# Rebuilt attention with masks, column halves and scaled probabilities in a three-layer block

## The chip, the cores and the metric

The kernel runs on one core of a Trainium2 chip, in fp32 throughout (weights are split into a high and a low part, so that three products in the engine's faster fp32 form give one of full precision). The metric is the device time of the launch in microseconds, the median of the runs shown.

## The reference

256 tokens of width 1024 pass through a first block (recurrent branch and a gated attention of 16 heads, merged, then a feed-forward) and two more layers (a block attention and a latent attention, each with a feed-forward). At 256 tokens all three attentions come down to causal softmax; the gated one has a selected and a window branch over the same 256 tokens, and a compressed branch with 15 keys:

```python
out = gb[..., 0:1] * o_cmp + gb[..., 1:2] * o_slc + gb[..., 2:3] * o_win       # gated
s = jnp.einsum("bhqd,bhkd->bhqk", qi, k) * scale                               # latent, block
s = jnp.where(key_pos[None, :] <= qpos[:, None], s, NEG_INF)
p = jax.nn.softmax(s, axis=-1)
o = jnp.einsum("bhqk,bkhd->bqhd", p, v)        # then o.reshape(B, S, H * dh) @ w_o
```

## The kernel before

Five engine programs are written out by hand, one `@block` function each, and meet only by semaphores. Each engine works in order. The weights come as 356 chunks of 128 x 1024 (`weight_stream`), through a ring of three raw buffers and one of six split ones: ScalarE writes the high part (`split_high`, L1264), VectorE the low part (`split_low`, L1720), TensorE multiplies (`split_product`, L607 to L609). The chunk's split is thus a duty of both engines everywhere, also inside the attentions.

An attention (`attention` in each of the engine programs) runs over heads. For a head, TensorE forms scores of two query tiles (128 x 128 and 128 x 256) in one bank, adds the mask as a bf16 product of identity and mask (L744), VectorE takes the negative row maxima (L1788, L1789), ScalarE the exponents with their sums (L1331, L1333), TensorE turns the three tiles of probabilities (L753), VectorE copies them out (L1795), and TensorE multiplies them, as the stationary operand, with the values of 64 columns (L765 to L767). Four heads share a bank of outputs, which VectorE multiplies by the inverse sums (`output`, L1802 to L1814; in the gated attention also by the gate, and adds the branches up). At the end TensorE turns the outputs, 16 tiles for each attention (`turn_output`, L802), ScalarE and VectorE write their high and low parts, and the output projection follows. The scores of two heads are formed side by side in row halves of the engine in the gated and the block attention (L737, L739), not in the latent one (L726, L727).

Between the heads stands other work. In the gated attention (32 items: 16 heads, two branches) halves of the merge-gate chunks (`merge_gates`, `mg`), with VectorE's `merge_scaled`; ahead of it the compressed branch, whose sums start at L2112. In the block attention the query and key tiles (`query_or_key`, 12 of 16 inside), which ScalarE copies out (`rope_operand`, L1589), TensorE rotates (`turn_rope`, L1108) and VectorE combines (`rope`, L2177 to L2185, one behind each head). In the latent attention the products of queries and keys (`query_product`, `key_product`), read by ScalarE (L1653, L1648) and VectorE (`query_rope`, L2256).

## Time and profile before

| | us |
|---|---|
| runs | 1176.53, 1176.68, 1176.81 (median 1176.68) |
| span of the profiled execution | 1173.1 |
| TensorE busy | 1141.7 (97%) |
| VectorE busy | 899.5 (77%) |
| ScalarE busy | 686.4 (59%) |
| DMA, mean | 162 GB/s read from HBM |

Busy times are unions of instruction spans; a matmul's span runs on while the next has started, so what one costs is the distance from its start to the next one's. In a timeline, columns are start, duration, engine, line, operation, result and operands with shapes, count, and in brackets idle time before and who ended it. A window's row gives its length and for each engine busy time and count, then the granted clock, the share of the DMA engines and GB/s.

### The profile page before, as it was taken

How to read it: one execution, taken by the hardware profiler on the slowest of the kernel's cores; microseconds unless marked ns; L12 is line 12 of the kernel's file. 1: busy time of each engine (PE TensorE's matmuls, PEld its weight loads, DVE VectorE, ACT ScalarE, POOL GpSimd, SP SyncE). 2: the span in 40 equal slices, each digit the busy share in tenths (PEclk: the TensorE clock that was granted, in tenths of full speed). 3: DMA queues.
4: the chain of work that ended last, by engine and by line, in shares of the span. 5: the costliest groups of instructions: out<-in, count | busy, mean ns of one | idle time of the engine just before them, and what ended most of it. 6: DMA issues, size and time to landing. Idle time of an engine off the chain costs nothing.

```text
span 1173.1 us, 25426 instructions
## 1 busy us (share of the span) xinstructions
PE 1141.7 (97%) x9673; PEld 1108.9 (95%) x9673; DVE 899.5 (77%) x1550; ACT 686.4 (59%) x1210; POOL 10.2 (1%) x13
## 2 busy tenths in 40 slices
PE   6999999999999999999999999999999999999997
PEld 6999999989999999999899899999998899999997
DVE  5788778678787998888777768776787777877774
ACT  6768764544556676556654456555565846655554
POOL 1000000000001000000000000000000000000000
PEclk9998999999999999999999999999999999999999
DMA  6675644521164676666453246766644423776661
GB/s 237 199 210 165 189 131 152 174 89 55 55 181 128 218 224 204 194 196 192 159 158 111 72 139 213 217 195 189 193 144 141 127 73 127 223 215 195 191 197 37
DMA packets 52923, 190.82 MB, mean 163 GB/s; under 512 B 6000, under 2 KB 6256, under 8 KB 52848
## 3 DMA queue, kind: packets, MB, share of 16 engines
q1 hardware_dynamic: 52416, 188.64, 52.5%
q8 instruction: 54, 0.88, 0.3%
q10 hardware_dynamic: 432, 1.12, 0.2%
q14 instruction: 21, 0.17, 0.0%
HBM read 188.69 MB, written 1.05 MB: 162 GB/s over the span
## 4 chain that ended last, share of the span: by engine, by line
PE 80%; DVE 8%; ACT 5%; DMA 4%; issue 2%; SPq 0%; DVEq 0%; ACTq 0%
PE bank L607 23%; PE bank L608 22%; PE bank L609 22%; DMA w_raw<-weight_stream 4%; DVE w_low L1720 3%; ACT w_high L1264 2%; PE bank L753 1%; DVE arena L1968 1%; PE bank L766 1%; PE bank L767 1%; PE bank L615 1%; PE bank L617 1%; PE bank L616 1%; PE bank L765 1%; PE bank L739 1%
## 5 line engine op out<-in xcount | busy, mean ns | idle before, releaser
L1720 DVE TENSOR_TENSOR w_low<-w_raw,w_high 128x1024 fp32r<-128x1024 f32 x356 | 434.6, 1224 | 148.0 <-ACT w_high L1264 144.2
L1264 ACT ACTIVATE w_high<-w_raw 128x1024 fp32r<-128x1024 f32 x356 | 375.1, 1058 | 265.3 <-PE bank L609 178.1
L607 PE MATMUL bank<-h_high,w_high 128*128 128x256 f32 x1760 | 495.1, 281 | 11.8 <-DVE h_low L1758 10.5
L608 PE MATMUL bank<-h_low,w_high 128*128 128x256 f32 x1760 | 488.5, 278 | 0.0
L609 PE MATMUL bank<-h_high,w_low 128*128 128x256 f32 x1760 | 488.5, 278 | 0.0
L607 PEld LDWEIGHTS bank<-h_high,w_high 128*128 128x128 f32 x1760 | 331.7, 188 | 13.7 <-issue 10.5
L608 PEld LDWEIGHTS bank<-h_low,w_high 128*128 128x128 f32 x1760 | 331.9, 189 | 0.4
L609 PEld LDWEIGHTS bank<-h_high,w_low 128*128 128x128 f32 x1760 | 331.7, 188 | 0.0
L607 PE MATMUL bank<-r_high,w_high 128*128 128x256 f32 x942 | 265.5, 282 | 3.8 <-ACT arena L1653 2.1
L608 PE MATMUL bank<-r_low,w_high 128*128 128x256 f32 x942 | 261.5, 278 | 0.0
L609 PE MATMUL bank<-r_high,w_low 128*128 128x256 f32 x942 | 261.5, 278 | 0.0
L607 PEld LDWEIGHTS bank<-r_high,w_high 128*128 128x128 f32 x942 | 177.9, 189 | 9.8 <-ACT arena L1653 3.6
L608 PEld LDWEIGHTS bank<-r_low,w_high 128*128 128x128 f32 x942 | 177.8, 189 | 0.2
L609 PEld LDWEIGHTS bank<-r_high,w_low 128*128 128x128 f32 x942 | 177.7, 189 | 0.0
L1846 DVE SCALAR_TENSOR_TENSOR arena<-arena,small 128x255 f32<-128x255 f32 (+1 forms) x184 | 87.9, 478 | 5.7 <-ACT arena L1359 2.4
L1331 ACT ACTIVATE arena<-bank,stats 128x128 f32<-128x128 f32 x64 | 23.4, 365 | 54.1 <-DVE stats L1789 53.9
L1359 ACT ACTIVATE arena<-arena,small 128x256 f32<-128x256 f32 x68 | 40.0, 589 | 13.7 <-DVE arena L1860 13.6
L1744 DVE TENSOR_TENSOR r_low<-arena,r_high 128x256 fp32r<-128x256 f32 (+1 forms) x96 | 41.9, 437 | 7.1 <-ACT r_high L1372 3.8
L1860 DVE TENSOR_TENSOR arena<-bank,rstd 128x256 f32<-128x256 f32 x68 | 28.8, 423 | 18.5 <-PE bank L609 18.4
L1795 DVE COPY arena<-bank 128x384 f32<-128x384 f32 x64 | 35.0, 550 | 3.8 <-PE bank L753 3.4
L1788 DVE TENSOR_REDUCE stats<-bank 128x1 f32<-128x128 f32 x64 | 18.3, 286 | 21.4 <-PE bank L744 21.4
L1372 ACT ACTIVATE r_high<-arena 128x256 fp32r<-128x256 f32 x68 | 27.8, 408 | 11.3 <-DVE arena L1884 10.2
(222 smaller groups left out, 1131.7 us busy)
## 6 DMA issues: line engine op xcount, KB each, us to landing
w_raw<-weight_stream SPq DMA_DIRECT2D x356, 512.0 KB, 4.2
x<-x_in SPq DMA_DIRECT2D x4, 256.0 KB, 6.0
small<-small_in ACTq DMA_DIRECT2D x1, 937.5 KB, 8.6
out<-arena SPq DMA_DIRECT2D x3, 256.0 KB, 2.5
out<-arena SPq DMA_DIRECT2D x1, 128.0 KB, 2.6
out<-arena ACTq DMA_DIRECT2D x1, 128.0 KB, 2.8
small<-small_in ACTq DMA_DIRECT2D x1, 30.5 KB, 4.0
```

Of the source, the lines that this page charges most:

```text
L607: mm(out_ap, wh, high, start=start, stop=False, skip_group_check=True)
L608: mm(out_ap, wh, low, start=False, stop=False, skip_group_check=True)
L609: return mm(out_ap, wl, high, start=False, stop=stop, skip_group_check=True)
L1264: fn(w_high[:, c % RING, :], w_raw[:, c % RAW, :], ACT.Copy).then_inc(high_ready, 1)
L1331: fn(probs[:, i % 3, 0:P], b[:, 0:P], ACT.Exp, bias=neg_max[:, h, 0:1], accum_out=sums[:, 0, h:h + 1])
L1359: fn(taps_g[:, j % 2, :], scaled_g[:, j % 2, :], ACT.Identity, scale=tap(f"fcw{n}", 2, k + j), bias=tap(f"fcb{n}", 0, k + j)).then_inc(tap ...
L1372: fn(r_high[:, j % SLOTS, :], hidden[:, j % 2, :], ACT.Copy).then_inc(hid_high, 1)
L1720: v.tensor_tensor(w_low[:, c % RING, :], w_raw[:, c % RAW, :], f(w_high[:, c % RING, :]), ALU.subtract).then_inc(low_ready, 1)
L1744: v.tensor_tensor(dst, src, f(high), ALU.subtract).then_inc(done, 1)
L1795: v.tensor_copy(probs_t[:, i % 2, :], use.turned_bank(i)[:, 0:3 * P]).then_inc(probs_copied, 1)
L1846: return v.scalar_tensor_tensor(dst[:, tokens:S], src[:, 0:S - tokens], tap(row, j), dst[:, tokens:S], ALU.mult, ALU.add)
L1860: v.tensor_tensor(scaled_g[:, slot, :], bank[slot][:, 0:S], rstd[:, :], ALU.mult).then_inc(g_scaled, 1)
```

## The change

- The mask product is gone from TensorE. VectorE adds the mask to the scores while it takes the maximum (`tensor_tensor_reduce`, L1806 and L1808 of the changed kernel, which writes the negated masked scores back to the bank).
- The probabilities are scaled before they are turned: VectorE forms the inverse sums of a pair and multiplies each head's two parts by them, and by the gate of the branch (L1815, L1822).
- The values become the stationary operand (64 columns), the turned probabilities the moving one. The two heads of a pair write partitions 0 to 63 and 64 to 127 of one bank, so that outputs arrive transposed; the gated branches and the compressed values add up in the same bank. The output transposes and the output scaling are gone. An output tile is split into high and low parts as soon as its pair is done.
- Work goes by pairs of heads; the copies of turned tiles are shared (even heads VectorE, odd heads ScalarE), in the latent attention VectorE makes all.
- Six probability buffers instead of three; scores in banks 4 to 6 in the two later attentions, turned tiles in 0 and 1, output in 2. All later query and key tiles share bank 3.
- The first three steps of the later output projections stand behind the last pairs. The compressed probabilities are scaled before their transposes, and the merge chunks 4 to 6 stand ahead of these. The zero halves of `k0` and `k1` are no longer written, and the constants are 128 columns wider.

Core of the diff:

```diff
...
-    put("mask", np.where(row[None, :] <= row[:, None], 0.0, NEG))
+    put("mask", np.concatenate([np.zeros((P, P)), np.where(row[None, :] <= row[:, None], 0.0, NEG)], 1))
...
-        ALL_BANKS = Banks((0, 1, 2), (3, 4), (5, 6))
-        BLOCK_BANKS = Banks((0, 1, 2), (3,), (4, 5), spare=6, spare_from=11)
-        LATENT_BANKS = Banks((0, 1, 2), (3,), (4, 5), spare=7, spare_from=12)
+        GATED_BANKS = Banks((0, 1, 2), (3, 4), 5)
+        LATER_BANKS = Banks((4, 5, 6), (0, 1), 2)
...
-            return bank[n if n < QK_AHEAD else 6][:, 0:S]
+            return bank[min(n, QK_AHEAD - 1)][:, 0:S]
...
-            return bank[{0: 2, 1: 3}.get(h, 6)][:, 0:S]
+            return bank[{0: 2, 2: 6}.get(h, 3)][:, 0:S]
...
-                def masked(i, b):
-                    mm(b[:, :].rearrange("p (a c) -> p a c", c=2 * P)[:, :, 0:P], ident_b[:, :],
-                       mask_b[:, :].unsqueeze(1).to_broadcast([P, 2, P]), start=False, stop=True,
-                       skip_group_check=True).then_inc(scores_ready, 1)
...
+            def attention(n, items, q, k, v, probs, probs_t, use, ready, between, compressed=None, rows=True):
+                done, base, per_output = NH * n, NH // 2 * n, 2 if compressed else 1
+
+                def scores(j):
+                    if j:
+                        pe.wait_ge(probs_ready, done + 2 * j - 1)
+                    products = [(i, t) for i in (2 * j, 2 * j + 1) for t in range(TT)]
+                    order = (0, 3, 1, 2) if rows else range(4)
+                    seen = set()
+                    for i, t in (products[m] for m in order):
+                        if i not in seen:
+                            ready(i)
+                        part = slice(HD * (i % 2), HD * (i % 2 + 1)) if rows else slice(0, P)
+                        at = slice(P * t, P * (2 * t + 1))
+                        ins = mm(of(use.scores, i)[:, at], q(i, t)[part, :], k(i)[part, 0:P * (t + 1)],
+                                 start=i not in seen, stop=i in seen, skip_group_check=True)
+                        if i in seen:
+                            ins.then_inc(scores_ready, 1)
+                        seen.add(i)
+
+                def turn(j):
+                    for i in (2 * j, 2 * j + 1):
+                        pe.wait_ge(probs_scaled, done + i + 1)
+                        if j:
+                            pe.wait_ge((even_copied, odd_copied)[i % 2], base + j)
+                        for part in range(3):
+                            ins = nc.tensor.transpose(bank[use.turned[i % 2]][:, part * P:(part + 1) * P],
+                                                      probs[:, i % 6, part * P:(part + 1) * P], ident)
+                        ins.then_inc(probs_turned, 1)
+
+                def values(j):
+                    output, first = j // per_output, j % per_output == 0
+                    o = bank[use.output]
+                    if first and output:
+                        pe.wait_ge(r_low_ready, R_O[max(n - 1, 0)] + output)
+                    if first and compressed:
+                        compressed(output, o)
+                        first = False
+                    pe.wait_ge(even_copied, base + j + 1)
+                    pe.wait_ge(odd_copied, base + j + 1)
+                    even, odd = (probs_t[:, i % 4, :] for i in (2 * j, 2 * j + 1))
+                    mm(o[0:HD, P:S], v(2 * j, 1), even[:, 2 * P:3 * P], start=first, stop=False, skip_group_check=True)
+                    mm(o[HD:P, 0:S], v(2 * j + 1, 0), odd[:, 0:S], start=first, stop=False, skip_group_check=True)
+                    mm(o[0:HD, 0:S], v(2 * j, 0), even[:, 0:S], start=False, stop=True, skip_group_check=True)
+                    mm(o[HD:P, P:S], v(2 * j + 1, 1), odd[:, 2 * P:3 * P], start=False, stop=True,
+                       skip_group_check=True).then_inc(pv_done, 1)
+
+                for j in range(items + 3):
+                    if j < items:
+                        scores(j)
+                    between(j, 0)
+                    if 2 <= j < items + 2:
+                        turn(j - 2)
+                    between(j, 1)
+                    if j >= 3:
+                        values(j - 3)
+                    between(j, 2)
...
+            def next_queries_and_keys(j, part):
+
+                n = QK_AHEAD + 2 * j
+                if j < NH // 2:
+                    if part == 0:
+                        if j == 0:
+                            turn_rope(QK_AHEAD - 1)
+                        if n < SIZE["qk1"]:
+                            query_or_key(n)
+                    elif n < SIZE["qk1"]:
+                        if part == 1:
+                            turn_rope(n)
+                            query_or_key(n + 1)
+                        else:
+                            turn_rope(n + 1)
...
+            def attention(n, items, probs, probs_t, use, behind_head=None, behind=None, odd_copies=True, per_output=1):
+                done, base = NH * n, NH // 2 * n
+
+                def exponents(i):
+                    act.wait_ge(max_ready, done + i + 1)
+                    if i >= 6:
+                        act.wait_ge(probs_turned, done + i - 5)
+                    b, h = of(use.scores, i), i % NH
+                    fn(probs[:, i % 6, 0:P], b[:, 0:P], ACT.Exp, bias=neg_max[:, h, 0:1], scale=-1.0,
+                       accum_out=sums[:, 0, h:h + 1])
+                    fn(probs[:, i % 6, P:3 * P], b[:, P:3 * P], ACT.Exp, bias=neg_max[:, h, 1:2], scale=-1.0,
+                       accum_out=sums[:, 1, h:h + 1]).then_inc(probs_ready, 1)
+
+                def output_high(j):
+                    if j % per_output == per_output - 1:
+                        act.wait_ge(pv_done, base + j + 1)
+                        which = max(n - 1, 0)
+                        fn(r_high[:, O_TILE[which][j // per_output], :], bank[use.output][:, 0:S],
+                           ACT.Copy).then_inc(r_high_ready, 1)
+
+                def copy_odd(j):
+                    act.wait_ge(probs_turned, done + 2 * j + 2)
+                    if j >= 2:
+                        act.wait_ge(pv_done, base + j - 1)
+                    fn(probs_t[:, (2 * j + 1) % 4, :], bank[use.turned[1]][:, 0:3 * P],
+                       ACT.Copy).then_inc(odd_copied, 1)
+
+                for j in range(items + 4):
+                    if j >= 4:
+                        output_high(j - 4)
+                    if j < items:
+                        for i in (2 * j, 2 * j + 1):
+                            exponents(i)
+                            if behind_head:
+                                behind_head(i)
+                    if behind:
+                        behind(j, 0)
+                    if odd_copies and 2 <= j < items + 2:
+                        copy_odd(j - 2)
+                    if behind:
+                        behind(j, 1)
...
+            def attention(n, items, probs, probs_t, use, behind, gate, odd_copies=False, per_output=1):
+                done, base = NH * n, NH // 2 * n
                 def row_max(i):
                     dve.wait_ge(scores_ready, done + i + 1)
                     b, h = of(use.scores, i), i % NH
-                    v.tensor_reduce(neg_max[:, h, 0:1], b[:, 0:P], AX.X, ALU.max, negate=True)
-                    v.tensor_reduce(neg_max[:, h, 1:2], b[:, P:3 * P], AX.X, ALU.max, negate=True).then_inc(max_ready, 1)
+                    v.tensor_tensor_reduce(out=b[:, 0:P], in0=b[:, 0:P], in1=par("mask", P, P), scale=-1.0,
+                                           scalar=3.0e38, op0=ALU.add, op1=ALU.min, accum_out=neg_max[:, h, 0:1])
+                    v.tensor_tensor_reduce(out=b[:, P:3 * P], in0=b[:, P:3 * P], in1=par("mask"), scale=-1.0,
+                                           scalar=3.0e38, op0=ALU.add, op1=ALU.min,
+                                           accum_out=neg_max[:, h, 1:2]).then_inc(max_ready, 1)
+
+                def inverse_sums(j):
+                    dve.wait_ge(probs_ready, done + 2 * j + 2)
+                    heads = slice(2 * j % NH, 2 * j % NH + 2)
+                    v.reciprocal(inv_sums[:, :, heads], sums[:, :, heads]).then_inc(inverse_ready, 1)
+
+                def scale_probs(j):
+                    dve.wait_ge(inverse_ready, base + j + 1)
+                    for i in (2 * j, 2 * j + 1):
+                        h, slot = i % NH, i % 6
+                        for t, part in ((0, probs[:, slot, 0:P]), (1, probs[:, slot, P:3 * P])):
+                            ins = v.tensor_scalar(part, part, inv_sums[:, t, h:h + 1], gate(i, t), ALU.mult, ALU.mult)
+                        ins.then_inc(probs_scaled, 1)
                 def copy_turned(i):
                     dve.wait_ge(probs_turned, done + i + 1)
-                    if i >= 2:
-                        dve.wait_ge(pv_done, done + i - 1)
+                    if i >= 4:
+                        dve.wait_ge(pv_done, base + i // 2 - 1)
+                    v.tensor_copy(probs_t[:, i % 4, :], bank[use.turned[i % 2]][:, 0:3 * P]).then_inc(
+                        (even_copied, odd_copied)[i % 2], 1)
+
+                def output_low(j):
+                    if j % per_output == per_output - 1:
+                        which, k = max(n - 1, 0), j // per_output
+                        at = O_TILE[which][k]
+                        low(r_low[:, at, :], bank[use.output][:, 0:S], r_high[:, at, :],
+                            r_high_ready, R_O[which] + k + 1, r_low_ready)
+
+                for j in range(items + 4):
+                    if j >= 4:
+                        output_low(j - 4)
+                    if 1 <= j <= items:
+                        inverse_sums(j - 1)
+                    for i in (2 * j, 2 * j + 1):
+                        if j < items:
+                            row_max(i)
+                    if 1 <= j <= items:
+                        scale_probs(j - 1)
+                    behind(j, 0)
+                    if 2 <= j < items + 2:
+                        copy_turned(2 * j - 4)
+                        if odd_copies:
+                            copy_turned(2 * j - 3)
+                    behind(j, 1)
...
+            def behind_block(j, part):
+
+                if j == 0 and part == 0:
+                    rope(QK_AHEAD - 1)
+                n = QK_AHEAD + 2 * j
+                if part and n < SIZE["qk1"]:
+                    rope(n)
+                    rope(n + 1)
...
+            def behind_latent(j, part):
+
+                if part == 0:
+                    for i in (2 * j, 2 * j + 1):
+                        if i + QUERIES_AHEAD < NH:
+                            query_rope(i + QUERIES_AHEAD)
+                else:
+                    for i in (2 * j, 2 * j + 1):
+                        for c in LATENT_SPLITS[i - 1]:
+                            split_low(c)
+                    if NH // 2 <= j < NH // 2 + 3:
+                        projection_split("wo2", j - NH // 2)
```

VectorE in the gated attention, before: the second head of a pair, a copy, and the scaling of four heads' outputs.

```order
L1788 TENSOR_REDUCE stats<-bank 128x1 [waits scores_ready]
L1789 TENSOR_REDUCE stats<-bank 128x1
L1795 COPY arena<-bank 128x384 [waits pv_done,probs_turned]
L1802 RECIPROCAL stats<-stats 128x2x4 [waits pv_done]
L1804 TENSOR_TENSOR stats<-stats 128x2x4 [waits dve_step]
L1811 TENSOR_TENSOR arena<-bank,stats 128x512 [waits dve_step]
L1812 TENSOR_TENSOR arena<-arena 128x2x256 [waits dve_step]
```

Now, in the second pair (`ISA ... 128x1` is the read of the accumulator):

```order
L1806 ISA bank,stats<-bank,small 128x128 [waits scores_ready]
L1806 ISA stats 128x1
L1808 ISA bank,stats<-bank,small 128x256
L1808 ISA stats 128x1
L1822 TENSOR_SCALAR arena<-arena,stats 128x128 [waits inverse_sums_ready]
L1822 TENSOR_SCALAR arena<-arena,stats 128x256
L1822 TENSOR_SCALAR arena<-arena,stats 128x128
L1822 TENSOR_SCALAR arena<-arena,stats 128x256
L1829 COPY arena<-bank 128x384 [waits probs_turned]
```

The output operations are gone, and four scalings stand between the maxima and the copy.

ScalarE in the block attention, before: exponents of one head, a rotation's operand, a split, exponents of the next.

```order
L1331 ACTIVATE arena,stats<-bank,stats 128x128 [waits probs_turned,max_ready]
L1333 ACTIVATE arena,stats<-bank,stats 128x256
L1589 ACTIVATE arena<-bank 128x256 [waits rope_done,chunk_used]
L1264 ACTIVATE w_high<-w_raw 128x1024 [waits chunk_used,chunk_loaded0]
L1331 ACTIVATE arena,stats<-bank,stats 128x128 [waits probs_turned,max_ready]
L1333 ACTIVATE arena,stats<-bank,stats 128x256
```

Now, in the sixth pair (L1317 writes the high part of an output, L1324 copies an odd head's turned tiles):

```order
L1317 ACTIVATE r_high<-bank 128x256 [waits pv_done]
L1308 ACTIVATE arena,stats<-bank,stats 128x128 [waits probs_turned,max_ready]
L1310 ACTIVATE arena,stats<-bank,stats 128x256
L1308 ACTIVATE arena,stats<-bank,stats 128x128 [waits probs_turned,max_ready]
L1310 ACTIVATE arena,stats<-bank,stats 128x256
L1589 ACTIVATE arena<-bank 128x256 [waits rope_done,chunk_used]
L1241 ACTIVATE w_high<-w_raw 128x1024 [waits chunk_used,chunk_loaded1]
L1324 ACTIVATE arena<-bank 128x384 [waits pv_done,probs_turned]
L1589 ACTIVATE arena<-bank 128x256 [waits rope_done,chunk_used]
L1241 ACTIVATE w_high<-w_raw 128x1024 [waits chunk_used,chunk_loaded2]
```

Both heads' exponents stand ahead of both operands.

VectorE in the latent attention, before: output scaling, a query, a split, a copy, maxima.

```order
L1802 RECIPROCAL stats<-stats 128x2x4 [waits pv_done]
L1814 TENSOR_TENSOR arena<-bank,stats 128x2x256 [waits dve_step]
L2256 SCALAR_TENSOR_TENSOR arena<-bank,small 64x256 [waits chunk_used]
L1720 TENSOR_TENSOR w_low<-w_raw,w_high 128x1024 [waits high_ready]
L1795 COPY arena<-bank 128x384 [waits pv_done,probs_turned]
L1788 TENSOR_REDUCE stats<-bank 128x1 [waits scores_ready]
```

Now, in the fifth pair, behind its maxima and the first head's scaling:

```order
L1822 TENSOR_SCALAR arena<-arena,stats 128x128
L1822 TENSOR_SCALAR arena<-arena,stats 128x256
L2284 SCALAR_TENSOR_TENSOR arena<-bank,small 64x256 [waits chunk_used]
L2284 SCALAR_TENSOR_TENSOR arena<-bank,small 64x256 [waits mla_query_products]
L1829 COPY arena<-bank 128x384 [waits pv_done,probs_turned] x2
L1738 TENSOR_TENSOR w_low<-w_raw,w_high 128x1024 [waits high_ready]
L1762 TENSOR_TENSOR r_low<-bank,r_high 128x256 [waits r_high_ready]
L1815 RECIPROCAL stats<-stats 128x2x2 [waits probs_ready]
```

Both queries stand ahead of both copies.

## Rows read from the trace of the kernel before

**Rows 1.** The windows of the three attention stages; busy us of each engine.
```profile
239.77:318.88 79.11, 78.14 (x687) 70.81 (x686) 62.70 (x149) 38.53 (x140) 0.00 (x0) 1.00 0.22 68
597.39:669.03 71.64, 69.33 (x573) 64.02 (x573) 57.04 (x121) 33.88 (x94) 0.00 (x0) 1.00 0.36 111
905.65:960.77 55.12, 52.08 (x413) 47.08 (x412) 42.59 (x86) 38.71 (x107) 0.00 (x0) 1.00 0.33 103
```

**Rows 2.** Timeline of TensorE, one pair of heads in the gated attention; start, us.
```profile
305.64 0.49 PE L737 MATMUL bank<-arena 64*128 64x128 f32 x4
...
306.49 0.39 PE L744 MATMUL bank<-mask_b,ident_b 128*128 128x256 bf16 x2
306.72 0.49 PE L753 MATMUL bank<-small,arena 128*128 128x128 f32 x3
307.05 0.33 PE L765 MATMUL bank<-arena 128*128 128x64 f32 x2
...
307.64 0.36 PE L607 MATMUL bank<-h_high,w_high 128*128 128x256 f32 x1
...
309.13 0.38 PE L753 MATMUL bank<-small,arena 128*128 128x128 f32 x2
```

**Rows 3.** Timeline of TensorE, products whose results lie in column halves, four calls merged.
```profile
205.29 1.09 PE L991 MATMUL bank<-small,stats 128*64 128x128 f32 x16
206.31 0.39 PE L607 MATMUL bank<-r_high,w_high 128*128 128x256 f32 x1
```

**Rows 4.** Groups by line and shape, TensorE and VectorE; busy us, mean ns.
```profile
L802 PE MATMUL bank<-small,arena 128*128 128x128 f32 x48 | 6.3, 273 | 0.0
...
L1758 DVE SCALAR_TENSOR_TENSOR h_low<-x,small,h_high 128x256 fp32r<-128x256 f32 x48 | 21.0, 479 | 5.1 <-ACT h_high L1306 5.0
...
L2011 DVE SCALAR_TENSOR_TENSOR arena<-arena 128x256 f32<-128x256 f32 x11 | 4.6, 421 | 1.4 <-ACT arena L1491 1.3
...
L2030 DVE TENSOR_SCALAR arena<-arena,small 128x256 f32<-128x256 f32 x8 | 2.8, 353 | 0.3
```

**Rows 5.** Timeline of VectorE in the gated attention, one head between its neighbours.
```profile
276.38 1.23 DVE L1720 TENSOR_TENSOR w_low<-w_raw,w_high 128x1024 fp32r<-128x1024 f32 x1
277.52 0.28 DVE L1788 TENSOR_REDUCE stats<-bank 128x1 f32<-128x128 f32 x1
277.72 0.41 DVE L1789 TENSOR_REDUCE stats<-bank 128x1 f32<-128x256 f32 x1
278.05 0.55 DVE L1795 COPY arena<-bank 128x384 f32<-128x384 f32 x1
```

**Rows 6.** Timeline of ScalarE in the gated attention, the exponents of a head.
```profile
265.46 0.37 ACT L1331 ACTIVATE arena<-bank,stats 128x128 f32<-128x128 f32 x1 [2.25 <-DVE stats L1789]
265.73 0.19 ACT L1331 ACTIVATION_READ_ACCUMULATOR arena<-bank,stats 128x1 f32 x1
265.82 0.46 ACT L1333 ACTIVATE arena<-bank,stats 128x256 f32<-128x256 f32 x1
```

**Rows 7.** Timelines of TensorE and VectorE in the block attention, from pair to pair.
```profile
614.75 0.49 PE L737 MATMUL bank<-arena 64*128 64x128 f32 x4
...
617.93 0.85 DVE L2185 TENSOR_TENSOR arena<-arena 64x256 f32<-64x256 f32 x2
...
620.95 0.65 PE L1108 MATMUL bank<-arena,small 128*128 128x256 f32 x2
...
621.64 0.42 DVE L2179 TENSOR_TENSOR arena<-bank,arena 128x256 f32<-128x256 f32 x1 [0.21 <-PE bank L1108]
...
624.36 0.49 PE L737 MATMUL bank<-arena 64*128 64x128 f32 x4
```

**Rows 8.** Timeline of VectorE ahead of the gated attention.
```profile
229.34 0.64 DVE L2112 TENSOR_REDUCE stats<-arena 128x32 f32<-128x480 f32 x1
```

**Rows 9.** Timelines of TensorE and VectorE in the latent attention, one query product.
```profile
946.21 0.38 PE L607 MATMUL bank<-r_high,w_high 128*128 128x256 f32 x1
...
947.55 0.43 DVE L2256 SCALAR_TENSOR_TENSOR arena<-bank,small 64x256 f32<-64x256 f32 x1 [0.26 <-PE bank L609]
```

505 lines of the change are left out of this document (181 added, 324 removed).

## The prediction

> **What bounds the kernel now.** I read the windows of the three attention stages first, because every edit lies in them [rows 1]. TensorE works for 78.1 of 79.1 us in the gated attention, 69.3 of 71.6 in the block attention, 52.1 of 55.1 in the latent one: about 6 us stand idle. It is the bound, so what leaves it shortens the program as long as nothing else takes its place. VectorE is the next: 62.7, 57.0 and 42.6 us, that is 79, 80 and 77 per cent. The question is therefore what the change takes from TensorE, and whether VectorE, which gets work in return, stays hidden. All times below are starts to starts within one execution of 1173.1 us, 3.6 below the median of 1176.7.
>
> **What leaves TensorE.** A pair of heads in the gated attention [rows 2]: scores 0.85 us (305.64 to 306.49), mask 0.23, turning three tiles 0.33 per head, values 0.59 per head (307.05 to 307.64), half a merge-gate chunk 1.49.
> - The mask: 32 pairs of heads (16 gated, 8, 8) by 0.23 = 7.4 us.
> - The 48 transposes of outputs [rows 4], at 0.11 each (three take 0.33 in [rows 2]) = 5.3 us.
> - The values: before 64 heads by 0.59 = 37.8. Now four products for a pair, 768 columns, in two column halves. The only products in halves in the trace are the spread roots: eight of 128 columns take 1.02 us, 205.29 to 206.31 [rows 3], 0.128 each; 768 columns are six such, 0.77 a pair, 24.6 in all, so 13.2 less. From above: the halves don't run side by side, twice that, 1.54 a pair, 11 us more than now.
> - Scores are the same columns in another order, taken at nothing. The compressed values become twice as many products of half the width, also nothing.
> The sum is 26 us, if TensorE alone counted.
>
> **What VectorE gets.** Units before: row maximum of a head 0.53 (277.52 to 278.05), split of a chunk 1.14 [rows 5].
> - The row maximum now also adds the mask and writes it back. The instruction listing shows each as two, the operation and the read of the accumulator. Columns are the same (128 and 256). VectorE has no such read in the trace; ScalarE's starts 0.09 before what follows (265.73 to 265.82) [rows 6]. I take 0.09 per read: 0.53 + 0.18 = 0.71 a head. From below: free, 0.53. From above: a read as long as its row says, 0.19, so 0.91.
> - Scaling: two TENSOR_SCALAR per head. One of 256 columns with one scalar from memory is 353 ns [rows 4], starts 0.08 before its end like its neighbours, so 0.27, and 0.07 less for 128: 0.47 a head. In the gated stage both scalars come from memory; one such costs 58 ns (479 against 421, [rows 4]), so 0.59 a head.
> - One reciprocal for a pair, 0.2 with its wait; one low part of 256 columns for an output tile, 0.33, where there was an output scaling of 0.9 (gated 1.8) per four heads.
> - ScalarE takes half the copies of turned tiles in two stages, 24 of 64; a row of 0.51 (0.55 long) leaves VectorE for each. In the latent stage VectorE keeps them.
>
> The Trainium skill (VectorE: DVE Perf Modes, section on the TRN2 errata) prices a Vector operation in SBUF at 58 cycles plus the columns over the mode's factor, at 0.96 GHz. That would be 0.19 us for 256 columns and 0.13 for 128, and the scaling of a gated pair 0.65 instead of 1.18. The sum below would then be about 7 us lower. The row of 353 ns speaks against it, and I keep the row.
>
> **Gated stage.** VectorE in two consecutive pairs: rows 4 x 0.71, scaling 4 x 0.59, reciprocals 0.4, two copies 1.06, one low part 0.33, one merge scaling 0.33, one split 1.15 = 8.5, 4.25 a pair. TensorE needs 0.85 + 0.66 + 0.77 + 1.49 = 3.8. Now it takes 4.52 (two heads and a half chunk, [rows 2] with both heads). So VectorE becomes the bound, and 0.27 a pair is left of 0.7. Along the program: the maxima start 1.55 us after the first scores, four pairs take 15.3 (the first wait for exponents), twelve take 51.0, the last turns, values and two half chunks 6.9 (with the 18 products of the output projection that lie in the window of before too): 74.8 against 79.1. Ahead of it the compressed values leave (3.6 us). But three merge chunks now follow each other in one bank, and the first must wait for VectorE's sum of the compressed probabilities, which starts at 229.34 [rows 8] as that chunk's predecessor ends, and for reciprocal, weights, two products and merge scaling behind it: 2.8 us where there is a wait of 0.2, and 0.7 at the next chunk. The first scores start 0.3 earlier. Together **4.7 us less**.
>
> **Block stage.** Here the order decides. Before, one query or key tile stands behind each head; a pair takes 9.61 us (614.75 to 624.36, [rows 7]), nearly all TensorE's. Now VectorE does both rotations behind both maxima, and TensorE starts the second turn only at the pair's end. The loop from that turn: 0.69 until its VectorE operation starts (620.95 to 621.64), 0.46, 0.85 for the two halves of a key [rows 7], split 1.15, reciprocal 0.2, both maxima 1.42, the exponents of the second head end 1.25 later (each head is 0.81 and a read of 0.11, and the second starts when the first is done), copy of the next operand 0.38, link 0.1: 6.5. Then the turn 0.3, the next tile 3.05, values 0.77: 10.6. With the low part, from the fifth pair, 10.9. The first pair comes to 9.8 against 8.4. Six pairs: 9.8 + 2 x 10.5 + 10.6 + 2 x 10.9 = 63.2, now 56.1. TensorE has 9.0 of work per pair and waits for the rest. The last two pairs get steps of the output projection as filler, and the output transposes are gone: 11.2 against 13.5. **4.8 us more**.
>
> **Latent stage.** VectorE keeps all copies. Both rotated queries of a pair use one bank, and the second product starts only when VectorE has read the first: 1.34 from a product's start to the reading (946.21 to 947.55, [rows 9]). The loop: maxima 1.42, scaling 0.95, first query 0.43, link and product 1.4, second query 0.45, copies 1.08, one split 1.2, low part 0.33, reciprocal 0.2 = 7.5. Three of the eight pairs hold two splits, 8.7. From the first scores to the last pair's maxima 54.0 us (2.1 + 6.5 + 7.6 + 8.7 + 8.7 + 7.4 + 7.4 + 5.6), and 12.5 to the last values, without the projection's 54 products that were not in the window before 6.1: 60.3 against 55.1. **5.2 us more**. The transposes saved there are TensorE's time beside an engine that is later.
>
> Sum: -4.7 + 4.8 + 5.2 = +5.3. Outside these stages nothing changes on TensorE; the constants grow by 64 KB and the memsets on GpSimd shrink, neither is waited for in the rows. 1176.7 + 5.3 = **1182.0 us**.
>
> The Trainium skill (TensorEngine Tiling (Array Packing), section on the PSUM bottleneck) says that tiling speeds up TensorE but not the evacuation of PSUM, which may then be the bottleneck, and that both ScalarE and VectorE should do it. It speaks against this change where VectorE keeps all copies, the latent stage; with every cost hidden it would be the 26 us less of the first sum.
>
> **Rivals.**
> 1. *The saving arrives.* VectorE runs ahead of TensorE and the loops close within its work: 1176.7 - 26 = 1151. For it: the windows leave VectorE 20 per cent. Against: in each stage the added work is 8 to 13 us, the free time 12 to 16, and it is split by waits.
> 2. *VectorE is cheaper than my rows.* Reads free and scalars from memory free: a gated pair 3.85, TensorE's own, so 6 us less there; each block pair 0.2 less and each latent one 0.36: 1182 - 6 - 1 - 3 = 1172. This is on the other side of no change; it decides from a maximum of 0.6 us a head on.
> 3. *The masked maximum is dear.* It reads PSUM and SBUF and writes PSUM; no row shows it. With 1.1 a head: 0.8 a pair, 16, 6 and 8 times: 1182 + 23 = 1205.
> 4. *The column halves don't run side by side.* 0.77 more a pair: in the gated stage TensorE is then 4.6 against 4.25 (+5), in the block loop four values lie on the path (+3): 1190. The edit would not do what it says.
>
> **Chances.** Forecast 0.48 (own range 1176 to 1189), rival 1 0.09, rival 2 0.2, rival 3 0.11, rival 4 0.12. The range takes in rival 2 with 4 us for the ends' fillers, rival 4, and a read of 0.19: 1166 to 1199. About 0.2 per cent, 2.4 us, is what can be told from no change. Faster: rivals 1 and 2, 0.27 with a share of the forecast's low end 0.03: 0.30. Within: 0.10. Slower: 0.60.
>
> **What would show it.** The masked maximum at 0.28 and 0.42 us with reads 0.09 apart; a pair of heads every 4.25 us in the gated stage with VectorE over 95 per cent; in the block stage TensorE idle about 1.5 us before each first turn of a pair, waiting for ScalarE's operand copy, and pairs of 10.6; in the latent stage idle TensorE before the second query product. Values of a pair in 0.77. If TensorE has no such waits, the loops are wrong and rival 1 or 2 holds; if a maximum takes over 0.9 a head, rival 3.

## The result and the profile after

The changed kernel takes 1182.48 us in the median of 8 runs (1178.55 to 1183.69), the kernel before 1176.74 (8 runs, 1176.31 to 1178.31) beside it. The ratio is 1.0048, with a 95% interval of 1.0033 to 1.0062: about 5.6 us, or half a per cent, slower. The forecast was 1182.0. The profiled execution has a span of 1178.0 us, 4.9 more than the 1173.1 of before; it is one of the quicker runs of the changed kernel (1179.93).

The first part of its page gives the busy time of each engine, its share of the span and its instructions:

```profile
PE 1127.6 (96%) x9449; PEld 1086.7 (92%) x9449; DVE 906.5 (77%) x1776; ACT 695.0 (59%) x1244; POOL 2.9 (0%) x9
```

TensorE's work fell by 14.1 us (1141.7 before), VectorE's rose by only 7.0 (899.5) and ScalarE's by 8.6. That the span grew all the same says that TensorE stands idle for longer: its idle stretches add up to 44.5 us in the timeline, 25.5 before. The windows of the three attention stages, from the first scores to the last values, answer to [rows 1] (length; busy us of TensorE, its weight loads, VectorE, ScalarE and GpSimd; clock, DMA share, GB/s):

```profile
239.66:314.37 74.71, 71.66 (x619) 62.36 (x619) 65.96 (x251) 49.23 (x166) 0.00 (x0) 1.00 0.24 74
591.50:669.25 77.75, 67.30 (x531) 58.74 (x531) 61.64 (x182) 38.26 (x107) 0.00 (x0) 1.00 0.36 109
903.78:961.09 57.31, 45.81 (x331) 39.24 (x332) 45.63 (x149) 39.16 (x110) 0.00 (x0) 0.97 0.31 96
```

TensorE is idle for 3.1 of 74.7 us in the gated attention, 10.5 of 77.8 in the block attention, 11.5 of 57.3 in the latent one, where it was 1.0, 2.3 and 3.0. The ends of a window don't hold the same work in both kernels (the gated window of the changed one holds 12 more of the output projection's products), so the table goes by points that both programs have: the first start on TensorE of the compressed scores (L1034, now L968), of each attention's scores, and of the next norm's spread (L708, now L673). "Again" is a second trace of the changed kernel (e8 below). Under "clock", the stretches at half clock that the changed kernel has in the section, in the first and the second trace.

| section, us | before | changed | again | forecast | clock |
|---|---|---|---|---|---|
| start to compressed scores | 220.1 | 217.9 | 218.0 | 0 | as before |
| to the gated scores | 19.6 | 21.8 | 22.2 | -0.3 | 2, 2 |
| gated attention, projections | 127.7 | 121.9 | 121.9 | -4.4 | 0, 0 |
| to the block scores | 229.9 | 229.9 | 229.9 | 0 | 0, 0 |
| block attention, projection | 96.9 | 100.7 | 102.6 | +4.8 | 0, 1 |
| to the latent scores | 211.4 | 211.5 | 211.7 | 0 | 0, 0 |
| latent attention, projection | 80.4 | 85.4 | 84.8 | +5.2 | 1, 1 |
| to the end | 187.1 | 188.8 | 188.4 | 0 | end |
| span | 1173.1 | 1178.0 | 1179.5 | +5.3 | |

Gain in the first stage, loss in the two others, as forecast. What no term of the prediction had is the last column. The windows before, in and behind two of these stretches, ahead of the gated attention, and the end of the program (the number ahead of the last two is the granted clock: 1.00 is 2.4 GHz, 0.50 is 1.2):

```profile
218.00:222.00 4.00, 4.00 (x38) 4.00 (x37) 2.06 (x4) 2.34 (x2) 0.00 (x0) 1.00 0.73 255
222.00:226.00 4.00, 4.00 (x23) 4.00 (x23) 1.69 (x4) 0.60 (x1) 0.00 (x0) 0.57 0.51 144
...
232.00:235.00 3.00, 3.00 (x18) 2.97 (x16) 0.02 (x1) 0.00 (x0) 0.00 (x0) 0.58 0.54 160
236.00:239.00 3.00, 3.00 (x27) 3.00 (x28) 1.33 (x2) 0.47 (x2) 0.00 (x0) 1.00 0.14 11
...
1168.00:1171.00 3.00, 2.45 (x13) 2.36 (x12) 0.17 (x1) 0.53 (x2) 0.00 (x0) 0.50 0.00 0
```

In the kernel before, the window 222 to 226 is at 1.00 with 36 instructions on TensorE, here there are 23 at 0.57. From the first to the last start, the 48 products from 221.38 on take 7.07 us, for 5.62 before: 1.4 lost. The wait ahead of the second stretch:

```profile
231.04 0.36 PE L577 MATMUL bank<-h_high,w_high 128*128 128x256 f32 x1 [2.31 <-DVE arena L2110]
```

Behind these 2.31 us, the 24 products of this chunk take 4.22 us up to the end of the last one (231.04 to 235.26), those of the next one 2.98, counted in the same way. The wait thus costs at least 3.5 us, not 2.3. How much a stretch takes from a section differs: the two traces with this stretch and without the one at 222 (e3 and e7 below) have 20.5 and 20.4 us there, e1, with neither wait nor stretch, 15.8. Of these 4.6 us, 2.8 are waits, so 1.8 go with the clock.

### The profile page after: what moved, and what is told of

Read it like the earlier page. It is cut to its first block, busy times and chain, and to the rows that moved or that the text cites. A ratio compares the mean times of both kernels' runs of the same rounds, so it can differ in the third digit from the quotient of the medians.

```text
span 1178.0 us, 25227 instructions
## 1 busy us (share of the span) xinstructions
PE 1127.6 (96%) x9449; PEld 1086.7 (92%) x9449; DVE 906.5 (77%) x1776; ACT 695.0 (59%) x1244; POOL 2.9 (0%) x9
## 3 DMA queue, kind: packets, MB, share of 16 engines
q10 hardware_dynamic: 432, 1.19, 0.3%
## 4 chain that ended last, share of the span: by engine, by line
PE 79%; DVE 11%; ACT 5%; DMA 2%; issue 2%; SPq 0%; DVEq 0%; ACTq 0%
PE bank L577 23%; PE bank L579 23%; PE bank L578 22%; DVE w_low L1738 4%; DMA w_raw<-weight_stream 2%; ACT w_high L1241 1%; PE bank L707 1%; PE bank L695 1%; PE bank L585 1%; DVE arena L1987 1%; PE bank L587 1%; PE bank L586 1%; PE bank L1050 1%; PE bank L724 1%; ACT h_high L1283 1%
## 5 line engine op out<-in xcount | busy, mean ns | idle before, releaser
L695 PE MATMUL bank<-arena 64*128 64x128 f32 (+3 forms) x256 | 36.0, 352 | 4.0 <-ACT arena L1310 3.6
L695 PEld LDWEIGHTS bank<-arena 64*128 64x128 f32 (+1 forms) x256 | 26.7, 191 | 12.1 <-issue 7.9
L1822 DVE TENSOR_SCALAR arena<-arena,stats 128x128 f32<-128x128 f32 (+1 forms) x128 | 36.0, 345 | 0.1
```

The lines of the kernel that those rows point to most:

```text
L695: ins = mm(of(use.scores, i)[:, at], q(i, t)[part, :], k(i)[part, 0:P * (t + 1)], start=i not in seen, stop=i in seen, skip_group_check=True)
L1822: ins = v.tensor_scalar(part, part, inv_sums[:, t, h:h + 1], gate(i, t), ALU.mult, ALU.mult)
```

## Gated attention: TensorE still sets it

A pair takes 3.92 or 4.32 us in turn (every second one holds compressed values too), 4.12 in the mean, where it was 4.52 [rows 2] and the forecast 4.25. One pair on TensorE, answering to [rows 2]: scores, half a merge-gate chunk, six turns, four value products.

```profile
263.52 0.92 PE L695 MATMUL bank<-arena 64*128 64x128 f32 x8
264.37 0.39 PE L577 MATMUL bank<-h_high,w_high 128*128 128x256 f32 x1
...
265.89 0.82 PE L707 MATMUL bank<-small,arena 128*128 128x128 f32 x6
266.64 0.32 PE L722 MATMUL bank<-arena 128*64 128x128 f32 x1
266.65 0.43 PE L723 MATMUL bank<-arena 128*64 128x256 f32 x1
...
267.44 0.49 PE L695 MATMUL bank<-arena 64*128 64x128 f32 x3
```

0.85, 1.52, 0.75, and 0.80 for the values (266.64 to 267.44), forecast at 0.77. The other kind of pair has 0.54 of compressed values in it, its half chunk and turns take 0.14 less, and it comes to 4.32. The mean is 4.12, and all of it is work: TensorE has no idle time from 263 to 296. VectorE beside it, answering to [rows 5]:

```profile
265.00 0.17 DVE L1815 RECIPROCAL stats<-stats 128x4 f32<-128x4 f32 x1
...
265.28 0.14 DVE L1806 DVE_READ_ACCUMULATOR2_ANT stats<- 128x1 f32 x1
265.28 0.47 DVE L1808 CUSTOM_DVE_ANT_0 bank<-bank,small 128x256 f32<-128x256 f32 x1
...
265.66 0.33 DVE L1806 CUSTOM_DVE_ANT_0 bank<-bank,small 128x128 f32<-128x128 f32 x1
...
265.91 0.47 DVE L1808 CUSTOM_DVE_ANT_0 bank<-bank,small 128x256 f32<-128x256 f32 x1
...
266.29 1.25 DVE L1822 TENSOR_SCALAR arena<-arena,stats 128x128 f32<-128x128 f32 x4
```

A masked maximum of a head is 0.63 us (265.66 to 266.29), forecast 0.71: the read (a row of 142 ns in the mean) of the accumulator starts with the following operation, both at 265.28 above, and costs little. The reciprocal is 0.09, the four scalings 1.16, forecast 0.2 and 1.18; the 0.65 that the prediction weighed against 1.18 did not come. VectorE is busy for 31.19 of the 32.96 us from 263.52 to 296.48, which are eight pairs: 3.9 a pair, not 4.25.

### e4: without the scaling

```diff
-                        for t, part in ((0, probs[:, slot, 0:P]), (1, probs[:, slot, P:3 * P])):
-                            ins = v.tensor_scalar(part, part, inv_sums[:, t, h:h + 1], gate(i, t), ALU.mult, ALU.mult)
+                        ins = v.tensor_scalar(inv_sums[:, 0, h:h + 1], inv_sums[:, 0, h:h + 1], 1.0, 1.0, ALU.mult, ALU.mult)
```

> The changed kernel without the scaling of probabilities in all three attentions (one operation on a single column per head stands in its place, so the outputs lack the inverse sums and the gates). Theory A (each stage is bound as its loop says): gated stage within 1 us of 74.7, since TensorE is busy all the time there at 4.12 us a pair; block stage within 1.5 us, since the scaling is not on its loop; latent stage 6 to 8 us less, since the 1.04 us are on the loop. In all 7 us less. Theory B (VectorE's load is what costs in every stage): 0.9 to 1.1 us less a pair everywhere, 25 us or more less.

1177.95 us, 1.0016 of before (1.0000 to 1.0032). The same stretch of the gated attention:

```profile
263.50:296.40 32.90, 32.90 (x290) 28.60 (x288) 23.71 (x108) 21.54 (x81) 0.00 (x0) 1.00 0.21 65
```

VectorE works 23.7 of 32.9 us where it worked 31.2, and the pairs are the same 4.12: TensorE is busy throughout. The block pairs stay too (9.6, 10.1, 10.0, 10.4, 10.7, 10.6; with scaling 9.7, 10.1, 10.0, 10.4, 10.6, 10.6). Theory A holds for both. In the latent attention it was too bold: the section is 82.2 us against 85.4 and 84.8, not 6 to 8 less, and only its fourth to sixth pairs are shorter. e3 says why.

### e7: both heads in one column half

```diff
-                    mm(o[HD:P, 0:S], v(2 * j + 1, 0), odd[:, 0:S], start=first, stop=False, skip_group_check=True)
+                    mm(o[0:HD, 0:S], v(2 * j + 1, 0), odd[:, 0:S], start=False, stop=False, skip_group_check=True)
...
-                    mm(o[HD:P, P:S], v(2 * j + 1, 1), odd[:, 2 * P:3 * P], start=False, stop=True,
+                    mm(o[0:HD, P:S], v(2 * j + 1, 1), odd[:, 2 * P:3 * P], start=False, stop=True,
```

> The changed kernel with the values of both heads of a pair written to partitions 0 to 63, none to 64 to 127 (the outputs of odd heads are thus mixed into those of even ones, the other half is undefined). Theory A (the two column halves work side by side, as the products of spread roots do): a pair's four value products take 1.5 us instead of 0.80; in the gated attention, where TensorE is busy all the time, a pair goes from 4.12 to 4.8, 11 us more; in the block attention the values are on the loop, 0.7 a pair in four pairs; in the latent one they are partly hidden. In all 14 to 20 us more. Theory B (the halves do not overlap, and 0.80 is what four products cost): no change.

1197.91 us (two runs), 1.0200 of before (1.0173 to 1.0226), 16 more than the changed kernel on the same chip: theory A. Value products of one pair:

```profile
267.93 0.43 PE L722 MATMUL bank<-arena 128*64 128x128 f32 x2
...
269.06 0.38 PE L725 MATMUL bank<-arena 128*64 128x128 f32 x2
269.37 0.49 PE L695 MATMUL bank<-arena 64*128 64x128 f32 x2
```

1.44 us (267.93 to 269.37) for the same four products. In two halves the first two start 0.01 us apart (266.64 and 266.65 above) and the four take 0.80 in all. The column halves do work side by side, and rival 4 is out.

### e9: the kernel before without its mask

```diff
-                    mm(b[:, P:3 * P], q(i, 1), k(i), start=False, stop=False, skip_group_check=True)
-                    masked(i, b)
+                    mm(b[:, P:3 * P], q(i, 1), k(i), start=False, stop=True, skip_group_check=True).then_inc(scores_ready, 1)
```

The same in `score_pair`.

> The kernel before without the mask product on TensorE (the mask is left out, so the softmax is over all 256 keys). Theory A (TensorE bounds the kernel before, so what leaves it comes off): 32 pairs of 0.23 us, 7.4 us less, gated stage 3.7, block and latent stage 1.8 each. Theory B (another engine is as late in the two later attentions, so a wait takes its place there): 3.7 us less in the gated attention and under 1 us in the two others together.

1172.23 us, 0.9980 of before (0.9962 to 0.9998): 2.4 us, neither theory's number. A pair of the gated attention:

```profile
278.37 0.49 PE L736 MATMUL bank<-arena 64*128 64x128 f32 x4
...
279.22 0.55 PE L748 MATMUL bank<-small,arena 128*128 128x128 f32 x3
```

The mask's 0.23 us are gone, but the three turns that follow the scores directly take 0.39 instead of 0.33 and a pair is 4.36 instead of 4.52: 0.16 less, where the prediction counted 0.23. In the block attention a pair is 9.53 instead of 9.61 to 9.70. Its rows show no new wait: the turns behind the scores again take 0.39 for 0.33 and one of the two tiles 3.03 for 2.93. The block section is 0.9 us shorter, the part from its end to the norm behind the latent attention 0.3. With 16 gated pairs at 0.16 that is 3.8 us: the term for the mask, 7.4 us, was about twice too large. (The gated section as a whole is only 0.7 us shorter in this trace, since its last 426 products take 50.3 us and in the trace before 48.6; the last section comes back to that.) A product of 0.23 between others, taken away, gives less than its distance from start to start.

## Ahead of the gated attention: a wait and its clock

### e1: one more bank for the merge-gate chunks

```diff
-            return bank[{0: 1, 2: 6, 3: 5}.get(i, 7)][:, 0:S]
+            return bank[{0: 1, 2: 6, 3: 5, 5: 6}.get(i, 7)][:, 0:S]
...
-                        pe.wait_ge(mg_scaled, 2 if i == 4 else i)
+                        pe.wait_ge(mg_scaled, {4: 2, 5: 3, 6: 5}.get(i, i))
```

> The changed kernel, but merge-gate chunk 5 lies in bank 6 instead of bank 7 (and chunk 6 waits for chunk 4's reading only). Theory A: the 2.31 and 0.61 us in which TensorE stands idle ahead of the gated attention (228.74 and 235.26 in the trace of the changed kernel) come from the one bank, and so does the stretch at half clock behind them (granted clock 0.50 from 233 to 235; the 24 products of chunk 5 take 4.22 us instead of 2.82). All goes: 4.3 us less, first scores at 235.4 instead of 239.66, and no window under 1.00 there. Theory B: the wait is VectorE's whole chain for the compressed branch, and moves to the transposes or to the first wait for exponents behind them: under 1.5 us less. Theory C: the clock falls there whatever the wait: 2.9 us less.

1176.07 us, 1.0001 of before (0.9988 to 1.0013). The section to the gated scores is 15.85 us, 5.9 shorter than in the first trace of the changed kernel:

```profile
222.00:226.00 4.00, 4.00 (x37) 4.00 (x35) 2.51 (x5) 1.67 (x2) 0.00 (x0) 1.00 0.32 113
...
230.00:234.00 4.00, 4.00 (x37) 3.68 (x35) 2.34 (x4) 2.16 (x3) 0.00 (x0) 1.00 0.60 178
```

TensorE is busy and at full clock in both. Theory A holds: 2.9 us of waits are gone, and with them the stretch behind. It is more than the 4.3 expected because the other stretch, 222 to 226, is missing here too; e6, e10 and e11, which have that one and neither of the waits, have a section of 17.0 us, so it is worth 1.2. The mean granted clock of a run fits: 0.991 in the ten runs of e1, 0.989 in the eight of the changed kernel. Over all traces the two stretches differ. A stretch behind the wait (at 228 to 236 us) is in all seven that keep the wait, 2.2 to 2.3 us long (the changed kernel, e2, e3, e4, e7, e8, e12), and in none of the five that don't (e1, e5, e6, e10, e11), so C falls. It begins 0.2 to 1.4 us behind the end of the wait, in e3 alone 0.3 us ahead of it. The one at 220 to 226 has no wait ahead of it; it follows the 32 compressed score products of 30 columns, and is there in eight of the twelve traces of kernels with the change, also in some without the wait (e6, e10, e11), and in e9's, but not in that of the kernel before. This trace has two stretches in the latent attention instead (918 to 922 and 935 to 939).

### e8: the changed kernel again

> The changed kernel once more, for a second trace of it and its time beside the kernels above on one chip. Theory A (its spread of 5 us from run to run comes from TensorE's clock, which falls to half for 3.4 us after its waits, at places that differ from run to run): the trace has three to five such stretches besides the one near 100 us and the one at the end, the kernel before has none; stages without one agree within 0.2 us between traces. Theory B (the spread is in the waits themselves): stages differ by over 0.5 us with the clock at 1.00.

1181.54 us, 1.0055 of before (1.0038 to 1.0072), and a span of 1179.5. The stretches lie at 221, 231, 658 and 934 us; sections without one agree within 0.2 us with the first trace (table above), the block section is 1.8 longer, with one stretch more. Sections that have the same number of them differ by 0.4 and 0.6, so their place matters too. The kernel before has none inside. So the stretches are theory A's, and the kernel with the longer waits has more of them. But the trace of the kernel before flatters it: its mean clock is 0.995, and 57 runs of it beside the experiments have 0.992 in the mean (0.987 to 0.996), 15 of the changed kernel 0.989. By these means the changed kernel spends some 8 us more of a run at half clock, which is about 4 us of time (an estimate: 0.0035 of 1178 us, divided by the 0.5 by which the clock falls). That they also make its times differ more from run to run isn't shown: over 8 runs it spreads by 5 us and the kernel before by 2, but in the 26 runs beside e1 to e4 the kernel before spreads by 6 (1171.3 to 1177.7).

## Block attention: the split ahead of the maxima

The loop of the prediction, in one pair of the changed kernel, on three engines: the second turn of a pair, VectorE's rotation behind it, its split, the maxima, ScalarE's exponents, the operand's copy, the first turn of the next pair.

```profile
620.74 0.70 PE L1050 MATMUL bank<-arena,small 128*128 128x256 f32 x2 [0.47 <-ACT arena L1589]
...
621.47 0.42 DVE L2192 TENSOR_TENSOR arena<-bank,arena 128x256 f32<-128x256 f32 x1 [0.33 <-PE bank L1050]
...
622.81 1.23 DVE L1738 TENSOR_TENSOR w_low<-w_raw,w_high 128x1024 fp32r<-128x1024 f32 x1
623.96 0.17 DVE L1815 RECIPROCAL stats<-stats 128x4 f32<-128x4 f32 x1
624.05 0.27 DVE L1806 CUSTOM_DVE_ANT_0 bank<-bank,small 128x128 f32<-128x128 f32 x1
...
624.79 0.37 ACT L1308 ACTIVATE arena<-bank,stats 128x128 f32<-128x128 f32 x1 [3.17 <-DVE stats L1808]
...
625.95 0.48 ACT L1310 ACTIVATE arena<-bank,stats 128x256 f32<-128x256 f32 x1
626.39 0.39 ACT L1589 ACTIVATE arena<-bank 128x256 f32<-128x256 f32 x1
...
626.84 0.70 PE L1050 MATMUL bank<-arena,small 128*128 128x256 f32 x2 [0.96 <-ACT arena L1589]
```

6.10 us from turn to turn, forecast 6.5; the difference is in the maxima and the reciprocal. TensorE stands idle ahead of the first turn for 0.96, waiting for L1589; the forecast was 1.5 and the same row. The pairs are 9.7, 10.1, 10.0, 10.4, 10.6 and 10.6 us against forecasts of 9.8, 10.5, 10.5, 10.6, 10.9 and 10.9.

### e2: the second split behind the maxima

```diff
-                    rope(n + 1)
+                    rope(n + 1, split=False)
...
                             row_max(i)
+                    if after_maxima:
+                        after_maxima(j)
                     if 1 <= j <= items:
                         scale_probs(j - 1)
```

Here `after_maxima` is the split that `rope` left out, in the block attention alone.

> The changed kernel, but in the block attention VectorE's split behind each second rotation of a pair stands behind both maxima of the next pair instead of ahead of them. Theory A (the loop of the prediction: turn, rotation, split, maxima, exponents, operand copy, turn): the split's 1.15 us leaves the loop, a pair takes 8.9 to 9.3 us instead of 10.0 to 10.6, TensorE's 0.9 to 1.3 us of idle time before each first turn of a pair shrink to 0.2 or less: 6 us less in all. Theory B (the exponents or the split on ScalarE hold the operand copy, or the split is needed at once by the next tile): under 2 us less, or a new wait at L577.

1174.31 us, 0.9995 of before (0.9979 to 1.0011). On VectorE the reciprocal and the maxima now follow the rotation at once:

```profile
621.83 0.85 DVE L2200 TENSOR_TENSOR arena<-arena 64x256 f32<-64x256 f32 x2
622.71 0.18 DVE L1815 RECIPROCAL stats<-stats 128x4 f32<-128x4 f32 x1
622.81 0.27 DVE L1806 CUSTOM_DVE_ANT_0 bank<-bank,small 128x128 f32<-128x128 f32 x1
...
624.01 1.22 DVE L1738 TENSOR_TENSOR w_low<-w_raw,w_high 128x1024 fp32r<-128x1024 f32 x1
```

The pairs are 9.7, 9.0, 9.0, 9.2, 9.6 and 9.6: 1.1 less from the second on, as long as the split that left the loop. Ahead of the first turns of a pair TensorE stood idle for 0.9 to 1.6 us; now there is one wait of 0.48 and no other. Theory A holds. The block section is 97.3 us against 100.7, with one stretch at half clock in it that the first trace of the changed kernel hasn't; the same edit in e5 and e10, without one, gives 95.0 and 95.1. That is under the 96.9 of the kernel before: the stage keeps what TensorE saves once the order on VectorE is right. No operation was made cheaper for it.

### e12: plain maxima

```diff
-                    v.tensor_tensor_reduce(out=b[:, 0:P], in0=b[:, 0:P], in1=par("mask", P, P), scale=-1.0,
-                                           scalar=3.0e38, op0=ALU.add, op1=ALU.min, accum_out=neg_max[:, h, 0:1])
+                    v.tensor_reduce(neg_max[:, h, 0:1], b[:, 0:P], AX.X, ALU.max, negate=True)
```

The same for the second part, and the exponents take the scores with a scale of 1.

> The changed kernel with plain row maxima on VectorE in place of the masked ones (the mask is left out altogether). Theory A (the masked maximum costs 0.63 us a head against 0.53, and lies on the loops of the two later attentions): 0.2 us less a pair there, 3 us less in all at most, nothing in the gated attention. Theory B (with the accumulator's reads and a write to PSUM the masked form is what makes VectorE late): 8 us less or more.

1177.09 us, 1.0020 of before (1.0005 to 1.0034). On VectorE, in the gated attention:

```profile
264.81 0.28 DVE L1806 TENSOR_REDUCE stats<-bank 128x1 f32<-128x128 f32 x1
265.00 0.41 DVE L1807 TENSOR_REDUCE stats<-bank 128x1 f32<-128x256 f32 x1
265.33 1.24 DVE L1819 TENSOR_SCALAR arena<-arena,stats 128x128 f32<-128x128 f32 x4
```

A plain maximum is 0.52 us (264.81 to 265.33), the masked one 0.63. Block pairs are 0.12 shorter, the gated section 0.3, the block section 0.3, the latent one 1.1 to 1.8. Rival 3 is out, and theory A is the nearer one. By the ratios e12 is 3.3 to 4.1 us quicker than the changed kernel, the sections make up about 2; the clock's share of the rest can't be told from one trace.

## Latent attention: one bank, and then ScalarE's row of duties

The prediction closed the loop over the single bank of the query products. One turn of it, in the changed kernel:

```profile
945.58 0.43 DVE L2284 SCALAR_TENSOR_TENSOR arena<-bank,small 64x256 f32<-64x256 f32 x1
...
946.15 0.36 PE L577 MATMUL bank<-r_high,w_high 128*128 128x256 f32 x1 [1.19 <-DVE arena L2284]
...
947.46 0.43 DVE L2284 SCALAR_TENSOR_TENSOR arena<-bank,small 64x256 f32<-64x256 f32 x1 [1.46 <-PE bank L579]
```

TensorE waits 1.19 us for VectorE to read the first query product, VectorE waits 1.46 for the second one. A pair is 7.2 us there, forecast 7.4. The second query products of pairs 4 and 5 wait for VectorE in the same way (2.45 and 0.76 us). Those of pairs 1 to 3 already wait for another engine in this trace, 1.62, 1.44 and 1.92 us; in the third:

```profile
922.55 0.39 PE L577 MATMUL bank<-r_high,w_high 128*128 128x256 f32 x1 [1.92 <-ACT arena L1665]
```

### e3: the first query ahead of the scalings

```diff
-                    for i in (2 * j, 2 * j + 1):
-                        if i + QUERIES_AHEAD < NH:
-                            query_rope(i + QUERIES_AHEAD)
+                    if 2 * j + 1 + QUERIES_AHEAD < NH:
+                        query_rope(2 * j + 1 + QUERIES_AHEAD)
```

The first query's reading stands in `after_maxima`.

> The changed kernel, but in the latent attention VectorE reads the first query product of a pair straight behind the two maxima, ahead of the four scalings. Theory A (the loop of the prediction, closed by the single bank of the query products): the 1.04 us of scaling leave the loop, a pair takes 6.2 us instead of 7.2, the idle time before the second query product (0.75, 1.19, and 2.45 with the clock at 0.50 behind it) goes: 6 to 8 us less in all. Theory B (VectorE's sum of work per pair, 5.7 us, or ScalarE's copy of the query behind the first exponents, sets the pair): under 2.5 us less.

1178.27 us, 1.0027 of before (1.0009 to 1.0045): 2.5 to 3.3 us less than the changed kernel by its two ratios, at the upper end of theory B and far from A. The latent section is 83.0 us, for 85.4 and 84.8. Pair by pair, from scores to scores:

| pair | 1 | 2 | 3 | 4 | 5 | 6 |
|---|---|---|---|---|---|---|
| forecast | 6.5 | 7.6 | 8.7 | 8.7 | 7.4 | 7.4 |
| changed | 6.0 | 6.4 | 7.5 | 9.3 | 8.0 | 7.2 |
| e3, query first | 6.0 | 6.4 | 7.5 | 8.1 | 7.5 | 6.4 |
| e4, no scaling | 6.1 | 6.4 | 7.5 | 8.1 | 7.5 | 6.4 |
| e6, copy ahead | 5.3 | 7.1 | 7.1 | 8.1 | 7.5 | 6.4 |
| e10, keys spread early | 5.3 | 5.8 | 6.2 | 8.1 | 7.5 | 6.3 |
| e11, odd copies on ScalarE | 5.3 | 5.8 | 6.2 | 7.6 | 7.0 | 5.9 |

The loop holds in pairs 4 to 6, and there moving the query is worth as much as leaving out the scaling. (Pairs 4 and 5 of the changed kernel also have its stretch at half clock, at 932 to 936 us; pair 6 is the clean one.) In pairs 1 to 3 neither does anything. In e3's trace the second query product of the third pair waits as before:

```profile
922.49 0.39 PE L577 MATMUL bank<-r_high,w_high 128*128 128x256 f32 x1 [1.92 <-ACT arena L1665]
```

L1665 is ScalarE's copy of the first query, behind the exponents and the spreading of the rotated key.

### e5: the three edits together

> The three edits of the kernels before together: chunk 5 in bank 6, the block attention's second split behind the maxima, the latent attention's first query read ahead of the scalings. Theory A (the three loops are independent, each stage keeps its own gain): from the first norm's milestones, 5.9 us less ahead of the gated attention, 5 less in the block attention (3.4 measured with one stretch at half clock of 1.7 in it), 1 to 2.4 in the latent one: 12 us less than the changed kernel in the same traces, 6 less than the kernel before. Theory B (a gain in one stage comes back as clock or as another wait further on): under 6 us less than the changed kernel. Either way each stretch at half clock in the trace costs up to 1.7 us, so that traces are compared with their number beside them.

1168.49 us, 0.9949 of before (0.9927 to 0.9971), with a span of 1166.6, 11.4 and 12.9 less than the two traces of the changed kernel: theory A. The sections to the gated scores, of the block and of the latent attention are 15.9, 95.0 and 82.7.

### e6: ScalarE copies the first query ahead of the exponents

```diff
                         for i in (2 * j, 2 * j + 1):
+                            if ahead_of_head:
+                                ahead_of_head(i)
                             exponents(i)
```

with `query_copy` of the even heads in it.

> The three edits, and in the latent attention ScalarE's copy of the first query product of a pair ahead of the exponents of its first head. In the trace with the query read early by VectorE, the second query product waits for that copy in six pairs (1.61, 1.44, 1.92, 1.56, 1.18 and 0.35 us: 8.1 in all), in the first three behind the exponents and the spreading of the rotated key. Theory A (that copy closes the loop now): the six waits fall to 0.3 or less, 5 to 7 us less than without this edit. Theory B (VectorE's maxima and scalings or the exponents set the pair, and only take the place of the copy): under 2 us less.

1168.92 us, 0.9947 of before (0.9927 to 0.9967), the same as e5: theory B. The waits took a new place. Now the first query product of the next pair waits:

```profile
904.80 0.39 PE L577 MATMUL bank<-r_high,w_high 128*128 128x256 f32 x1 [2.44 <-ACT arena L1668]
911.39 0.39 PE L577 MATMUL bank<-r_high,w_high 128*128 128x256 f32 x1 [2.06 <-ACT arena L1668]
```

for ScalarE's copy of the second query (L1668), which starts at 904.37 in a row without a gap behind this:

```profile
900.75 1.05 ACT L1640 ACTIVATE arena<-arena 64x1024 f32<-64x1024 f32 x1
901.83 1.06 ACT L1241 ACTIVATE w_high<-w_raw 128x1024 fp32r<-128x1024 f32 x1
902.79 0.35 ACT L1309 ACTIVATE arena<-bank,stats 128x128 f32<-128x128 f32 x1
...
903.59 0.76 ACT L1663 ACTIVATE arena<-bank 64x256 f32<-64x256 f32 x2
904.37 0.38 ACT L1668 ACTIVATE arena<-bank 64x256 f32<-64x256 f32 x1
```

### e10 and e11: the row made shorter

```diff
-                if i in (0, 2, 4):
-                    spread_key(1 + i // 2)
...
             latents_high(2, 5)
+            for i in (1, 2, 3):
+                spread_key(i)
```

> The four edits (chunk 5 in bank 6, second split behind the maxima, first query read by VectorE ahead of the scalings and by ScalarE ahead of the exponents), and the three spreadings of the rotated key (1.08 us each on ScalarE, between the exponents of the first three pairs of the latent attention) ahead of that attention. Theory A (ScalarE's row of duties closes the loop of the first three pairs): each is 1.0 us shorter, the waits of 2.44, 2.06 and 1.60 us ahead of the first query product of a pair shrink by as much; 3 us less than without it. Theory B (they delay ScalarE's copies of keys and queries ahead of the attention, and the gain is given back there): no change.

1165.27 us, 0.9916 of before (0.9893 to 0.9938). The two waits are shorter by 1.2 us each:

```profile
904.00 0.39 PE L577 MATMUL bank<-r_high,w_high 128*128 128x256 f32 x1 [1.22 <-ACT arena L1670]
909.38 0.38 PE L577 MATMUL bank<-r_high,w_high 128*128 128x256 f32 x1 [0.88 <-ACT arena L1670]
```

The second and third pair are 1.2 and 0.8 us shorter, the first is not. The section ahead of the latent attention is 1.1 us longer (the first scores wait 1.34 for VectorE), the latent one 2.1 shorter than in e6. So ScalarE's row is the loop, as in theory A, but half of the gain is given back ahead of it, as in B. By the ratios e10 is 3.6 us better than e6, with an interval of about as much either way; the edit's own sections make up 1.0 of it, and the traces differ by a stretch at half clock in the block attention besides. e11 adds this:

```diff
-            attention(3, NH // 2, probs2, probs_t2, LATER_BANKS, behind_latent, lambda i, t: 1.0, odd_copies=True,
+            attention(3, NH // 2, probs2, probs_t2, LATER_BANKS, behind_latent, lambda i, t: 1.0,
...
-                      odd_copies=False)
+                      odd_copies=True)
```

(the first in VectorE's program, the second in ScalarE's)

> The five edits of the kernel before in this list, and in the latent attention too ScalarE copies the odd heads' turned tiles instead of VectorE. Theory A (the prediction's reading of that stage: VectorE keeps all copies and sets the pairs with two splits): 0.52 us leave VectorE in each of eight pairs, 2 to 4 us less than without it. Theory B (ScalarE closes the loop in that stage, since exponents, copies of queries and keys and splits stand in one row there): a copy more on ScalarE, 0.45 us a pair, makes it 1 to 4 us more.

1164.47 us, 0.9913 of before (0.9891 to 0.9935). Pairs 4 to 6 are 0.5 us shorter each, the time of one copy (0.52); the section is 78.0 us, 2.3 less than in e10 and 2.4 less than in the kernel before. The medians are only 0.8 apart; the trace of e11 has one stretch at half clock more than that of e10, in the block attention. The loop over VectorE is what set those pairs, as forecast. This version is 10.6 us faster than the kernel before in the medians of one chip, and 16 to 17 faster than the changed kernel by the ratios. The rule of the Trainium skill that the prediction weighed (TensorEngine Tiling (Array Packing), section on the PSUM bottleneck: let both engines evacuate) agrees with this run, where the second engine is worth 0.5 us a pair.

## Why the prediction was right, and where it was so by luck

The sum was 1182.0 and the median is 1182.48. The signs of the three stages hold, and so do the loops in the block attention and in half of the latent one. That the number is met to half a microsecond is luck: errors of 1 to 2.4 us, in five places, cancel: -1.4 and +2.4 around the first stage, -1.0 in the second, -2.2 at the start, +1.7 at the end. What weighs most is the granted clock, a term that the prediction did not have. In the trace it adds about 3 us ahead of the gated attention (5.9 that e1 takes away, less 2.9 of waits) and 1.7 at the end (below), and the stretch in the latent attention stands in its 5.0. Together this is more than 4.7 us, about the whole difference of the two traces (4.9); with the clock of the trace before, the changed kernel would have been 1 us slower at most, not 5.3 (an estimate, from the table with the start at nothing and 1.2 us or more for the latent stretch). Of the medians' 5.6 us, by the mean clocks under e8, it is about 4.

1. **Gated stage**, forecast 4.3 less in the window, measured 5.8 less for the same work. The step "VectorE becomes the bound" failed: the row maximum was costed at 0.71 by taking ScalarE's accumulator read as VectorE's (it is 0.63), and TensorE's 3.8 left out the 0.27 a pair of compressed values, which the forecast took off ahead of the stage (3.6 us) and put nowhere. A pair is 4.12 us of TensorE's work and 3.9 of VectorE's, and it is TensorE that sets it (e4).
2. **Ahead of it**, waits of 2.8 and 0.7 were forecast, 2.31 and 0.61 measured (e1 removes both). The clock behind the wait and the stretch ahead of it, 3.0 us together, were in no term: instead of 0.3 less, the section is 2.1 more.
3. **Block stage**, +3.8 for +4.8. The loop and who waits in it are right (e2); the maxima and the reciprocal were 0.3 us too dear each time round.
4. **Latent stage**, +5.0 and 0.2 ahead of it for +5.2. Right in pairs 4 to 6 (e3, e11). In pairs 1 to 3 the step that failed is the choice of the loop: ScalarE's row, with the spreading of the key in it, set them (e6, e10). They came out 0.5 to 1.2 us under the forecast each, pairs 4 and 5 0.6 above it, and that the section as a whole is near is chance. What the one stretch at half clock costs in this section is part of the 5.0.
5. **Start and end.** The start is 2.2 us earlier, which is not the change: e9, built from the kernel before, reaches the same point at 218.6, the kernels with the change at 216.7 to 219.8. At the end the last 32 norm products take 4.9 us instead of 3.6 and the four behind them 1.2 instead of 0.7: in both traces the clock falls near 1167.6 us, and the changed kernel, 3.2 us later, still has them to do.
6. **TensorE's saving**, 26 us in the first sum: its busy time fell by 14.1. The values gave what was forecast (0.80 a pair for 0.77), the mask about half (e9). That the rest is busy time which the half clock stretches is argued, not shown.

Of the rivals, the first would need the loops closed, and with six edits of order, banks and engines (e11) 11 of its 26 us arrive. The second was half right: the reads are nearly free and TensorE sets the gated pairs, but scalars from memory cost what the forecast said (1.16), a pair took 4.12 and not 3.85, and the loops of the two other stages hold at the measured costs too. The third and the fourth are out (e12, e7).

## What to carry to other kernels

When work moves to an engine that is free a fifth of the time, look for the loop it lands in, not for the share: here 0.11 us more for each head's maxima cost about 2 us over all three stages (e12), and one split of 1.15 us ahead of the maxima in place of behind them cost 5.7 us in one of them (100.7 against 95.0). Follow the loop for every engine in it and for the first pairs apart, since one duty that only they have (the spreading of the key) can make another loop the longer one. A wait of TensorE can cost more than its length, here at least 3.5 us for 2.3, so a spare bank is worth trying first where the longest wait is.

## What the runs showed of the hardware

- A stretch at the granted clock of 0.50 costs 1.2 to 2.3 us: 24 products take 4.22 us in one instead of 2.98, 48 take 7.07 instead of 5.62 from first to last start, a block section 1.8 to 2.3 more (e8, e2), the section ahead of the gated attention 1.2 to 1.8. Between 107 and 1167 us the trace of the kernel before has none, those of the changed one three and four. One came behind or at the end of the wait of 2.2 to 2.3 us in seven traces of seven; one came behind 32 products of 30 columns, with no wait, in eight of twelve, and in e9 one twice as long. What decides in the second case is left open.
- A Vector operation with an accumulator shows its read as a row of 142 ns, but the next operation starts with it: masked and plain maxima differ by 0.11 us a head, with the mask's reading and the writing back in it.
- Between the gated attention's last values and the next norm, 414 products of the two projections take 47.2 us in some traces (the changed kernel, e6, e8, e11, e12) and 48.9 in others (e1 to e5, e7, e10), at the same clock of 1.00 and with nothing waited for. The kernel before and e9 differ likewise (48.6 and 50.3 for 426). This is 1.6 us of a run's time, and no run explains it.
